# Split weights kept as word pairs: the high and the low half of each weight beside each other in one buffer

## The reference

```python
h2 = rmsnorm(x, norm2_g[l])
x = x + jnp.square(jax.nn.relu(h2 @ w_up[l])) @ w_down[l]
...
def swiglu(h, w_gu, w_down):
    g, u = jnp.split(h @ w_gu, 2, axis=-1)
    return (jax.nn.silu(g) * u) @ w_down
...
    x = x + FFN_RES_WEIGHT * rms_norm(swiglu(rms_norm(x, ng[0]), ffn_w_gu_2[l, 0], ffn_w_down_2[l, 0]), ng[1])
```

## Time and profile before

| what | value |
|---|---|
| time, median of 2 runs | 1475.64 us (1472.47 and 1478.81) |
| span of the profiled execution | 1470.6 us |
| TensorE matmul busy | 1401.7 us, 95%, 11538 instructions |
| TensorE weight load busy | 1358.3 us, 92% |
| VectorE busy | 922.4 us, 63% |
| ScalarE busy | 732.0 us, 50% |
| GpSimd busy | 192.7 us, 13% |
| HBM traffic | 241.67 MB read, 165 GB/s over the span |
| mean granted TensorE clock | 0.982 of full speed |

### The profile page before, as it was taken

The page is one execution under the profiler, slowest core; times in us unless marked ns, Lnnn a source line. Parts: engine busy times, 40 slices in busy tenths (PEclk is TensorE's granted clock), DMA queues, the critical chain, the costliest instruction groups (busy, mean ns, idle before and its releaser), DMA issues.

```text
span 1470.6 us, 28247 instructions
## 1 busy us (share of the span) xinstructions
PE 1401.7 (95%) x11538; PEld 1358.3 (92%) x11538; DVE 922.4 (63%) x1368; ACT 732.0 (50%) x1205; POOL 192.7 (13%) x210
## 2 busy tenths in 40 slices
PE   5899899999999999999998999999999989899998
PEld 5878799999999999998898999999999987899998
DVE  7998786666535665556765665556564467565644
ACT  7712755544435454455446454455444364554443
POOL 0465000022000111013101111011110010111100
PEclk9899899999999999999999999999999989999999
DMA  9223324455554555544342555544555341345551
GB/s 372 105 103 116 127 86 174 159 204 185 194 185 160 177 195 191 195 173 155 135 144 99 190 197 189 198 172 172 188 198 199 146 170 58 109 178 195 192 200 58
DMA packets 36815, 244.33 MB, mean 166 GB/s; under 512 B 4208, under 2 KB 5360, under 8 KB 8816
## 3 DMA queue, kind: packets, MB, share of 16 engines
q1 hardware_dynamic: 34992, 238.17, 44.7%
q10 hardware_dynamic: 1728, 4.81, 0.9%
HBM read 241.67 MB, written 1.05 MB: 165 GB/s over the span
## 4 chain that ended last, share of the span: by engine, by line
PE 81%; DVE 9%; ACT 5%; issue 2%; POOL 2%; DMA 1%; SPq 0%; DVEq 0%; ACTq 0%; POOLq 0%
PE ps L1891 49%; PE ps L1931 26%; DVE wlo L1083 3%; PE ps L2114 1%; PE ps L2140 1%; ACT whi L592 1%; DVE alo L1478 1%; PE ps L2130 1%; DMA xtok<-in_xt 1%; POOL pr L1809 1%; POOL pr L1808 1%; PE ps L2019 1%; ACT junk L829 1%; DVE yr L1456 0%; ACT pP L782 0%
## 5 line engine op out<-in xcount | busy, mean ns | idle before, releaser
L1083 DVE TENSOR_TENSOR wlo<-raw,whi 128x1024 fp32r<-128x1024 f32 (+1 forms) x434 | 505.1, 1205 | 273.3 <-ACT whi L592 273.2
L1891 PE MATMUL ps<-ahi,whi 128*128 128x256 f32 x2112 | 599.5, 284 | 32.1 <-DVE wlo L1083 18.0
L592 ACT ACTIVATE whi<-raw 128x1024 fp32r<-128x1024 f32 (+1 forms) x434 | 427.2, 1032 | 368.8 <-PE ps L1931 188.1
L1891 PE MATMUL ps<-alo,whi 128*128 128x256 f32 x2112 | 595.4, 282 | 0.0
L1891 PE MATMUL ps<-ahi,wlo 128*128 128x256 f32 x2112 | 594.0, 281 | 0.0
L1891 PEld LDWEIGHTS ps<-ahi,whi 128*128 128x128 f32 x2112 | 403.1, 191 | 38.2 <-issue 23.5
L1891 PEld LDWEIGHTS ps<-alo,whi 128*128 128x128 f32 x2112 | 402.8, 191 | 0.7 <-issue 0.7
L1891 PEld LDWEIGHTS ps<-ahi,wlo 128*128 128x128 f32 x2112 | 401.9, 190 | 0.0
L1829 POOL TENSOR_TENSOR hlo<-fh,hhi 128x256 f32 (+3 forms) x104 | 86.1, 828 | 756.2 <-ACT hhi L899 545.5
L1538 DVE TENSOR_TENSOR fa<-ps,r 128x512 f32<-128x512 f32 x104 | 71.9, 692 | 171.1 <-PE ps L1891 170.9
L1931 PE MATMUL ps<-whi,hhi 128*128 128x256 f32 x960 | 149.1, 277 | 0.0
(11 more groups left out here) (350 smaller groups left out, 1362.9 us busy)
## 6 DMA issues: line engine op xcount, KB each, us to landing
raw<-in_w_gu SPq DMA_DIRECT2D x88, 1024.0 KB, 4.8
raw<-in_w_fd SPq DMA_DIRECT2D x44, 1024.0 KB, 4.8
raw<-in_w_up SPq DMA_DIRECT2D x16, 1024.0 KB, 4.8
raw<-in_w_dn SPq DMA_DIRECT2D x16, 1024.0 KB, 4.8
raw<-in_w_ret SPq DMA_DIRECT2D x13, 1024.0 KB, 4.8
raw<-in_w_mg SPq DMA_DIRECT2D x8, 1024.0 KB, 4.9
raw<-in_w_o SPq DMA_DIRECT2D x8, 1024.0 KB, 6.3
raw<-in_w_mem SPq DMA_DIRECT2D x4, 1024.0 KB, 4.7
```

Of the source, the lines that this page charges most:

```text
L592: nc.scalar.activation(whi[:, m % SPL, c], raw[:, n % RAW, c], ACT.Copy).then_inc(S("w_hi"), 1)
L1083: ins = tt(wlo[:, m % SPL, c], raw[:, n % RAW, c], whi[:, m % SPL, c].bitcast(F32), ALU.subtract)
L1891: ins = mm(dst, lhsT, rhs, start=k == 0 and p == 0, stop=k == kt - 1 and p == len(pairs) - 1)
```

## The change

`whi` and `wlo` become the even and the odd words of one buffer, `wpair`. Its size is that of both together. All code that reads or writes `whi` and `wlo` stays as it is, but each access pattern now steps by two words (8 bytes): the writes of ScalarE (L592) and VectorE (L1083), VectorE's read of the high half, the weight loads of `products` and the moving reads of `down` and of the three `tokens` units. Counts, order, waits and transfers are those of before; `raw` and the activations stay contiguous. Within the pair buffer a slot is 16 KB long for each partition, where before each of the two halves had slots of 8 KB.

```diff
         raw = sb("raw", [P, RAW, UNIT])
-        whi = sb("whi", [P, SPL, UNIT], F32R)
-        wlo = sb("wlo", [P, SPL, UNIT], F32R)
+        wpair = sb("wpair", [P, SPL, UNIT, 2], F32R)
+        whi, wlo = wpair[:, :, :, 0], wpair[:, :, :, 1]
         at_x0 = base[0]
```

## The result

The changed kernel takes 1892.01 us (1890.59 and 1893.42) against 1475.64: 1.282 times as long, 95% interval 1.2776 to 1.2863. The profiled execution has a span of 1888.8 us and a time of 1890.59 us. The forecast was 1844 us; the measured time lies 48 us above it and 2 us above the upper end of the range, 1890. Those 2 us are within the noise of two runs (the interval is 1885 to 1898 us); the 48 are not.

The account below looks back on a forecast made before the run. TensorE's pace was taken to bound the kernel. 1475.64 us plus 368 for moving weight reads, with nothing for weight loads, splits or the rest, gave 1844 us; the eight-in-ten range was 1466 to 1890 us.

Parts of the forecast that it names:

- What bounds the kernel: Whole kernel: TensorE, busy 95% of the span, sets the time by its pace in long matmul runs.
- Part 1: Moving weight reads in down and tokens: 3600 matmuls slow to 217 ns each, 368 us more.
- the float32 row: Float32 matmuls of L1891, 256 columns in 379 ns, 217 ns between starts; taken as the price of strided moving reads.
- Part 2: Weight loads of L1891: 6576 loads at a step of two words cost nothing; upper bound 658 us.
- the scattered 720: Matmuls with moving weights outside the w_dn and four w_fd runs, 101 ns more each, 73 us.
- upper bound of 658 us: Weight loads: 100 ns more on each of 6576 if they paid the price of L2079's row.
- Part 3: ScalarE's writes, VectorE's read and write in the splits: zero cost taken, bounds 0 and 160 us.
- Part 4: All else: slots 16 KB apart in place of 8, same total size and addresses, no wait or transfer added.
- (a): Moving port manages with two words of a group: no change, 1476 us, 1455 to 1500; chance 0.25.
- (b): Moving and stationary reads both halve: 2502 us, or 2134 with the weight loads alone; chance 0.11.
- (d): TensorE pays 10 to 60 ns for each moving matmul: 1512 to 1692 us; chance 0.09.
- (c): TensorE untouched but splits slower by 37 to 160 us: 1513 to 1636, say 1560 us; chance 0.07.

Follow-up runs that it names:

- e4: Computation left out, single accesses timed at several steps and run lengths: 256 moving float32r words took 120.0 ns at step 1, 226.7 at step 2.
- e2: Kernel before, with word pairs only in units whose weights are the moving operand, all others contiguous: 1876.52 us, ratio 1.2718.
- e3: Kernel before, with word pairs only in units whose weights are the stationary operand: 1489.03 us, ratio 1.0091.
- e7: Computation left out, moving reads timed by run start, word count and type: runs of 4 of 8 straddling two groups took 227 ns and more.
- e8: The changed kernel, with moving weights read in order 0, 4, 2, 6 and stored to match: 1498.26 us, ratio 1.017 to the kernel before.
- e1: Kernel before, with both halves of a unit in one 16 KB slot, each contiguous, no step: 1476.62 us, ratio 0.9995.
- e5: Kernel before, with halves alternating in runs of four words where weights move, contiguous halves in the other units: 1490.3 us, ratio 1.0083.
- e9: Computation left out, 256 moving float32r words timed in other orders: 111.7 ns with the streams apart, 120.0 in order.
- e11: Computation left out, more orders of 256 adjacent moving words timed: 135 to 143 ns with two groups per stream, 223 to 240 with four.
- e10: Kernel before, with moving weights of down read in order 0, 128, 1, 129 and stored to match: 1467.5 us against 1475.9, ratio 0.9941.

## Why the prediction was right, and where it was wrong

**What bounds the kernel** was right: TensorE's pace set the time before and after, and the uncovered splits did not grow.

**Part 1** had the mechanism and the count right and the price wrong. The step that failed is "31 starts take 7.10 - 0.38 = 6.72 us, 217 ns each. That is my price": the pace of a strided moving read is 230 ns in the kernel, 227 to 230 by itself (e4), not that of the float32 row, which reads its words in order. With the moving reads alone changed the kernel pays 399.6 us (e2), where part 1 had 368: that is 32 of the 48 us, and the loads of part 2 are 12 more (e3), which leaves 4, within the noise. In its terms: w_dn was to cost 76 us and cost 176.64 - 90.46 = 86; the four w_fd runs were to cost 219 and cost some 246 (61.6 in each); the scattered 720 were put at 73, and what the span leaves for them and all the rest is 70 (418 less 86, 246 and the 16 of part 2). That last agreement is in part luck: 720 matmuls at 230 ns would cost some 82 us if none were covered, so a price too low and cover that was left out cancel. The extra is in the stream: 0.885 ns a word at step 2, against 0.833 at step 16 (e7). Why step 2 pays that stays open.

The reading behind it, a fixed price of about 1.6 ns for a group of four words, is right for weight loads, ScalarE, VectorE, float32 and bfloat16 (e4, e7), and half right for the float32r moving operand. It named step 2 rightly and would have been far off for step 4, at some 430 ns in place of 233. I had one stream where the rows ask for two (e8).

**Part 2** was small but not nothing: it was put at zero, on the reading that two words of a group take just as long as the group, and it is the second term that failed. The loads grew by 10 ns and the pace went to 120: 4.6 us in w_up, 4.2 and three times 2.25 in gate-up, some 16 in the long runs, 12 us in all by e3 alone, where w_dn got 3 us faster, as it did in e1. The upper bound of 658 us was never near.

**Part 3** was right for VectorE. ScalarE's write takes 1149 ns in place of 1052. By itself it goes from 0.95 to 0.99 us in pace, 0.04 of those 0.10 us (e4); where the rest comes from isn't shown. The slack covers it, so it cost nothing.

**Part 4** was right: e1 shows that the slot distance costs nothing. What it shows besides, paces that change places between w_up and w_dn, was allowed for as a gain and was none.

Of the signs that were to show it right, L1891 at 276 to 284 ns, VectorE at 1230 and the share of TensorE came true. L1931 at 425 ns (379), 528 of them in 121.46 us (115), loads at 198 (188) and L592 at 1149 (1052) did not.

**The rivals.** (a), no change, falls on e2. Its rule, two hits in a 16-byte line for full bandwidth (the Trainium skill, "SBUF — State Buffer", Specifications (TRN2)), agrees with e4 for loads (120.0 ns at steps 1 and 2), ScalarE (0.95 and 0.99 us) and VectorE (1.14 us at both), and e7 shows the 16 bytes. For the float32r moving operand the runs decide against it: two words of each line, read in order, take 226.7 ns where four take 120.0 (e4). (b) falls on e3, (d) on the size, 112 to 117 ns more for each moving matmul where it had 10 to 60. (c) falls on the durations of VectorE. The rule of adjacent pairs beside it (the Trainium skill, "Vector Engine (DVE) Microarchitecture Reference", section 5.2) is not borne out at a step of two words: e4 has 1.13 to 1.14 us for 1024 columns at steps 1 and 2. For a word that stands alone the section has 1.71 to 1.76 ns a column. The 1.82 us of a write at step 4, 1.78 ns a column, are near that; a read at step 4, 1.88 us or 1.84 ns, is somewhat above.

**The range** failed by 2 us at its upper end. The price was given 20 us of room downwards and, beside the 37 us for exposed splits, 9 upwards, though its row was of another type and had no step; and part 2 was given none.

## What to carry to other kernels

Ask of every operand how many bytes of each aligned 16 it uses, and at what rate its port takes words; a step that is free for a load or for VectorE can halve the rate of a float32r matmul (e4), and if TensorE's pace sets the time all of it counts. Interleave moving operands in aligned runs of four words (e5), or read them so that every other element stays in a line (e8). A price taken from an instruction of the right rate but another access form was 13 ns of 230 too low here; leave room above such a price.

## What the runs showed of the hardware

- A float32r moving operand behaves as two streams of alternate words. Each costs 0.83 ns a word or 1.67 ns for a new 16-byte group, whichever is more (e4, e7, e9). All steps that were measured from 2 to 16 words take 217.8 to 233 ns for 256 columns.
- Order 0,4,2,6 of the even words runs at 116 ns (e9) where 0,2,4,6 runs at 227 (e4).
- In order, 256 adjacent words take 120 ns in the probes and 113.4 to 117.8 in the kernel; with the two streams in different groups 111.7, and 512 words 216 against 227 (e11). In the kernel this was worth 0.6% (e10).
- A stream that goes back and forth between two groups takes 135 to 143 ns, between four 223 to 240 (e11).
- Weight loads of contiguous columns last 208 ns in place of 188 to 192 beside a strided moving operand, in the kernel and in e4.
